# A recurrence in rounds: side work of three engines moved off the edges between rounds, and one masking operation for both heads

## The reference

```python
def step(state, inp):
    r_t, w_t, k_t, v_t, a_t, b_t = inp
    sa = jnp.einsum('bhvk,bhk->bhv', state, a_t)
    state = state * w_t[:, :, None, :] + sa[..., None] * b_t[:, :, None, :] + v_t[..., None] * k_t[:, :, None, :]
    y = jnp.einsum('bhvk,bhk->bhv', state, r_t)
    return state, y
...
y_f, bonus_f = direction(0)
y_b, bonus_b = direction(1)
y = y_f + y_b
mean = jnp.mean(y, axis=-1, keepdims=True)
var = jnp.mean(jnp.square(y - mean), axis=-1, keepdims=True)
yn = ((y - mean) * lax.rsqrt(var + RWKV_GN_EPS)).reshape(b, s, d) * lnx_w.astype(F32) + lnx_b.astype(F32)
out = (yn + (bonus_f + bonus_b).reshape(b, s, d)) * g.astype(F32)
```

## Time and profile before

| | |
|---|---|
| median of 3 runs | 2835.26 us (2833.51 to 2841.53) |
| profiled execution, its own time | 2841.87 us |
| its span | 2840.1 us |
| mean granted clock | 0.991 |
| PE busy | 2705.1 us (95%) |
| DVE, ACT, POOL busy | 1459.3, 1262.3, 1127.4 us |
| the recurrence | about from 787.3 to 1264.1 us of the span |

### The profile page before, as it was taken

One profiled execution on the slowest core, in us unless ns is written; L12 is line 12 of the kernel. 1 busy time (PEld: TensorE's weight loads), 2 busy tenths in 40 slices (PEclk: granted clock), 3 DMA queues, 4 the chain that ended last, 5 costly groups with the idle time before them and its releaser, 6 DMA issues.

```text
span 2840.1 us, 54966 instructions
## 1 busy us (share of the span) xinstructions
PE 2705.1 (95%) x23332; PEld 2152.4 (76%) x23332; DVE 1459.3 (51%) x2561; ACT 1262.3 (44%) x2296; POOL 1127.4 (40%) x634
## 2 busy tenths in 40 slices
PE   7999999979989999989999999899999999999999
PEld 5668888857777777777888877577777777788887
DVE  7956886056767777754888203712222224234410
ACT  5764434234556555544443325634444454422221
POOL 4124444533543333314444444043333443544443
PEclk9999999999999999999999999999999999999999
DMA  5112332322300000012233232032221322333322
GB/s 165 49 38 89 97 94 90 97 91 89 96 19 11 8 7 8 6 46 77 94 97 90 92 100 67 15 111 77 75 75 56 106 84 81 97 91 96 95 88 77
DMA packets 63460, 208.88 MB, mean 74 GB/s; under 512 B 11248, under 2 KB 11504, under 8 KB 62832
## 3 DMA queue, kind: packets, MB, share of 16 engines
q1 hardware_dynamic: 60704, 193.10, 22.0%
q0 software_dynamic: 1936, 10.91, 1.1%
q10 hardware_dynamic: 576, 1.35, 0.2%
HBM read 199.95 MB, written 4.19 MB: 72 GB/s over the span
## 4 chain that ended last, share of the span: by engine, by line
PE 83%; DVE 11%; ACT 3%; issue 2%; DMA 0%; POOL 0%; SPq 0%; DVEq 0%; ACTq 0%
PE banks L1672 22%; PE banks L1674 21%; PE banks L1673 21%; PE banks L779 6%; PE banks L788 1%; PE banks L1816 1%; DVE low L539 1%; ACT arena L1119 1%; DVE arena L1532 1%; DVE arena L2661 1%; PE banks L845 1%; PE banks L871 1%; PE banks L1709 1%; PE banks L1792 1%; PE banks L1864 1%
## 5 line engine op out<-in xcount | busy, mean ns | idle before, releaser
L312 POOL TENSOR_TENSOR low<-arena,high 128x1024 fp32r<-128x1024 f32 (+1 forms) x376 | 876.5, 2332 | 1323.3 <-ACT high L303 1320.0
L1672 PE MATMUL banks<-high,high 128*128 128x512 f32 (+1 forms) x2752 | 1093.5, 397 | 38.2 <-POOL low L312 21.2
L1674 PE MATMUL banks<-high,low 128*128 128x512 f32 (+1 forms) x2752 | 1082.4, 393 | 0.0
L1673 PE MATMUL banks<-low,high 128*128 128x512 f32 (+1 forms) x2752 | 1082.3, 393 | 0.0
L303 ACT ACTIVATE high<-arena 128x1024 fp32r<-128x1024 f32 (+1 forms) x376 | 382.0, 1016 | 802.6 <-PE banks L1674 801.3
L1672 PEld LDWEIGHTS banks<-high,high 128*128 128x128 f32 x2752 | 519.5, 189 | 170.0 <-POOL low L312 18.0
L1674 PEld LDWEIGHTS banks<-high,low 128*128 128x128 f32 x2752 | 519.4, 189 | 121.4
L1673 PEld LDWEIGHTS banks<-low,high 128*128 128x128 f32 x2752 | 519.9, 189 | 119.0 <-issue 1.9
L2556 DVE TENSOR_TENSOR arena<-banks,arena 128x512 f32<-128x512 f32 x48 | 33.1, 692 | 425.2 <-PE banks L1674 424.1
L779 PE MATMUL banks<-arena 64*64 64x64 f32 x5632 | 207.3, 222 | 37.1 <-ACT arena L1119 31.5
L2690 DVE SCALAR_TENSOR_TENSOR arena<-arena 128x511 f32<-128x511 f32 x88 | 237.2, 2695 | 3.1
(11 more groups left out here) (294 smaller groups left out, 2994.6 us busy)
## 6 DMA issues: line engine op xcount, KB each, us to landing
arena<-weights SPq DMA_DIRECT2D x302, 512.0 KB, 3.5
arena<-weights SPq DMA_DIRECT2D x48, 448.0 KB, 3.2
arena<-weights SPq DMA_DIRECT2D x28, 256.0 KB, 2.6
arena<-tables POOLq DMA_DIRECT2D x5, 448.0 KB, 3.7
arena<-x_t SPq DMA_DIRECT2D x4, 512.0 KB, 5.8
x_spill<-arena POOLq DMA_DIRECT2D x1, 2048.0 KB, 9.3
arena<-small_weights POOLq DMA_DIRECT2D x16, 128.0 KB, 2.7
arena<-x_spill POOLq DMA_DIRECT2D x1, 2048.0 KB, 8.8
```

The costliest lines, as they stand in the source:

```text
L312: pool.tensor_tensor(lo[:, 0:n], ring[w % RING][:, 0:n], hi[:, 0:n].bitcast(F32), ALU.subtract).then_inc(w_low, 1)
L1672: pe.matmul(dst, hi[:, c], x[0], start=kt == 0, stop=False)
L1673: pe.matmul(dst, hi[:, c], x[1], start=False, stop=False)
L1674: mm = pe.matmul(dst, lo[:, c], x[0], start=False, stop=kt == kts_of[t] - 1)
```

## The change

Five orders change and one operation is merged.

- VectorE: `exclusive` moves from the end of rounds 1 and 2 (behind the new state) to the step U5, behind `centre`. In round 3 `r_` goes ahead of `a_`: r_0 behind M, a_0 behind U2, r_1 behind U4, a_1 behind U5 (ahead of `y_out`).
- VectorE: both heads' NT are masked in one operation of 128x768 elements instead of two of 128x384 (`both_j` spans two PSUM banks).
- TensorE: `merge(i, 1)` goes ahead of `aux(i, 1)`.
- ScalarE: `sigmoid` of sa0 and sa1 and `shifted_bonus` move from ahead of the copies of S1 to behind those of S2; the exponentials of round 3 come later by a step, in the order er1, ei1, ea1, F.

```diff
-    PRE_ACT = ["ksq", "rn", "sw0", "sa0", "sw1", "sa1", "er0", "ea0", "ei0", "er1", "ea1", "ei1", "F"]
+    PRE_ACT = ["ksq", "rn", "sw0", "sa0", "sw1", "sa1", "er0", "ea0", "ei0", "er1", "ei1", "ea1", "F"]
...
-    INV_DVE = two("DT", "D", "M", "U2", "U3", "U4", "U5", "U6")
+    INV_DVE = ["DT"] + two("D", "M", "U2", "U3", "U4", "U5", "U6")
...
             if off:
+                merge(i, 1)
                 aux(i, 1)
-                merge(i, 1)
                 for h in range(2):
                     grow(i, h, 5)
                 aux_gate(i)
...
-                if c == 1 and more:
-                    sigmoid(j + 1, "sa0", PP[1])
-                if c == 2 and more:
-                    sigmoid(j + 1, "sa1", PP[1])
-                if c == 3 and j:
-                    shifted_bonus(j - 1, PP[1])
                 for h in range(2):
                     ev("S1", h, flat(R.P2[:, h, :, :]), 256)
...
                 for h in range(2):
                     ev("S2", h, flat(R.P4[:, h, :, :]), 256)
-                if c == 3 and more:
-                    factor(j + 1, "er1")
+                if c == 1 and more:
+                    sigmoid(j + 1, "sa0", PP[1])
+                if c == 2 and more:
+                    sigmoid(j + 1, "sa1", PP[1])
+                if c == 3 and j:
+                    shifted_bonus(j - 1, PP[1])
                 for h in range(2):
                     ev("S3", h, flat(R.D[:, h, :, :]), P)
                 if c == 0 and more:
                     norm_k(j + 1)
                 if c == 3 and more:
-                    factor(j + 1, "ea1")
+                    factor(j + 1, "er1")
...
                 if c == 3 and more:
                     factor(j + 1, "ei1")
-                    factor(j + 1, "F")
+                    factor(j + 1, "ea1")
                 for h in range(2):
                     ev("Q1", h, flat(R.P2[:, h, :, :]), 256)
...
+                if c == 3 and more:
+                    factor(j + 1, "F")
...
         def a_(j, d):
             ra.wait(dve, j, f"ea{d}")
-            dve.scalar_tensor_tensor(R.AR[j % 2][d][:, :, 0, :], c8(ea[d]), -1.0, c8(kkn), ALU.mult, ALU.mult)
+            rd.inc(dve.scalar_tensor_tensor(R.AR[j % 2][d][:, :, 0, :], c8(ea[d]), -1.0, c8(kkn), ALU.mult, ALU.mult), f"AR{d}")
 
         def r_(j, d):
-            rd.inc(dve.tensor_tensor(R.AR[j % 2][d][:, :, 1, :], c8(er[d]), c8(R.r[:, j, :]), ALU.mult), f"AR{d}")
+            ra.wait(dve, j, f"er{d}")
+            dve.tensor_tensor(R.AR[j % 2][d][:, :, 1, :], c8(er[d]), c8(R.r[:, j, :]), ALU.mult)
...
             elif at_ == (1, "U5") and more:
                 centre(j + 1, 0)
-            elif at_ == (1, "U6") and more:
                 exclusive(j + 1, 0)
...
             elif at_ == (2, "U5"):
                 if more:
                     centre(j + 1, 1)
+                    exclusive(j + 1, 1)
                 if j >= 2:
                     z_gate(j - 2, PP[1])
-            elif at_ == (2, "U6") and more:
-                exclusive(j + 1, 1)
             elif at_ == (3, "M") and more:
+                r_(j + 1, 0)
+            elif at_ == (3, "U2") and more:
                 a_(j + 1, 0)
-            elif at_ == (3, "U2") and more:
-                r_(j + 1, 0)
             elif at_ == (3, "U3") and prev:
                 y_normed(j - 1)
             elif at_ == (3, "U4") and more:
-                a_(j + 1, 1)
                 r_(j + 1, 1)
-            elif at_ == (3, "U5") and prev:
-                y_out(j - 1, PP[1])
+            elif at_ == (3, "U5"):
+                if more:
+                    a_(j + 1, 1)
+                if prev:
+                    y_out(j - 1, PP[1])
...
                 p2.wait(dve, i, "NT")
-                for h in range(2):
-                    d2.inc(dve.tensor_tensor(R.NM[:, h, :, :], PJ[h][:, 0:P].unsqueeze(1).to_broadcast([P, 3, P]), below, ALU.mult),
-                           f"DT_{h}")
+                d2.inc(dve.tensor_tensor(R.NM, both_j[:, :, 0:P].unsqueeze(2).to_broadcast([P, 2, 3, P]),
+                                         below.unsqueeze(1).to_broadcast([P, 2, 3, P]), ALU.mult), "DT")
```

More of the change, by code:

```diff
@@ L661, in build @@
     PI, PJ, PX, PP = psum[0:2], psum[2:4], psum[4:6], psum[6:8]
-    both_x, both_p = (banks[:, 1024 * k:1024 * k + 1024].rearrange("p (h b) -> p h b", h=2) for k in (2, 3))
+    both_j, both_x, both_p = (banks[:, 1024 * k:1024 * k + 1024].rearrange("p (h b) -> p h b", h=2) for k in (1, 2, 3))
     hf = lambda i: slice(64 * i, 64 * i + 64)
@@ L1106, in act_rwkv @@
                 copy(name, 7)
-                for n in ("er1", "ea1", "ei1", "F"):
+                for n in ("er1", "ei1", "ea1", "F"):
                     factor(0, n)
@@ L1460, in dve_rwkv @@
         for d in range(2):
+            r_(0, d)
             a_(0, d)
-            r_(0, d)
         wait_tile(dve, tiles_of["rw_g1"][-1])
@@ L1583, in dve_rwkv @@
                 new_state(1)
-            if off:
-                spread(i, "U6")
         y_bonus(KT - 1)
```

## The result

The changed kernel takes 2849.4 us, median of five runs (2846.29 to 2853.42), against 2835.9 before: ratio 1.0047, 95% interval 1.0036 to 1.0058. It is 13.5 us slower, where I had forecast 7 us faster. The profiled execution took 2853.42 us (span 2851.6), and the mean granted clock fell from 0.991 to 0.986.

What follows compares the result with a forecast made beforehand. TensorE, 83% of the chain of waits, was taken as the bound. 0.92 us for each of seven pairs gave 6.4, less 0.3 plus 0.9 made 7.0 us: from 2835.26 to 2828.3 us, range 2820 to 2836.

Steps and rivals of the forecast that it cites:

- In rounds 1 and 2 VectorE is later still, so nothing follows.: Moved sigmoids start `aux_left` and TensorE's queue behind it 0.1 to 0.2 us later; claimed cost in rounds 1 and 2: none.
- Rival 3, the clock: New idle ahead of merge drops the clock in all six gate rounds, 3.9 us each: 12 us slower, 2848; chance 0.06.
- the longest new idle stretch, some 0.6 us: Argument against clock falls: TensorE's new idle ahead of merge is no longer than what the other five gate rounds bore.
- The signs of being wrong: U5 later than merge + 1.5, merged mask over 1.0 us, round 3 longer, or clock falls in more than two rounds.
- The edges: Ends of rounds 1 and 2, where `exclusive` leaves the path: gains of 0.18 us into round 2, 0.39 into round 3.
- The sum per pair: Gain per pair of heads: 0.35 + 0.39 for edges and round 2, 0.13, -0.1 and 0.15 for rounds 0, 1, 3: 0.92 us.
- Round 0: Merge can start 0.6 us earlier, but a table load delays the copy of Q1: gain 0.13 us instead of 0.6.
- the shifted bonus: Moved behind the copies of S2 on ScalarE, it makes `aux_left` start later and costs 0.17 us in round 3.
- The merged mask: One VectorE operation takes some 0.9 us instead of 1.01 for two; hidden behind TensorE's own queue, so gain 0.
- Aux behind merge: Aux fills TensorE's wait for Q1 but outlasts it: U5 at merge + 1.4 to 1.5 us, against 1.17 before.
- Round 3: `r_1` takes 0.7 us ahead of GpSimd's L1236, `a_1` waits for L1237; U6 at 1084.7 against 1084.84, gain 0.15 us.
- The lock between VectorE and GpSimd: The operation that starts first blocks the other to its end; `y_square` meets 0.4 us less of it, U4 0.6 earlier.

Runs made afterwards that it cites:

- e1: Changed kernel with the sa0 and sa1 sigmoids back ahead of the copies of S1; 2828.07 us, 0.9966 of before.
- e4: Kernel before with only the two sigmoids moved behind the copies of S2; 2844.62 us, 1.0027 of before.
- e6: Changed kernel with five extra TensorE turns that nobody reads ahead of merge in rounds 1 and 2; 2831.83 us, 0.9985 of before.
- e2: Changed kernel with aux(i, 1) back ahead of merge(i, 1); 2830.91 us, 0.9984 of before.
- e14: Changed kernel with the sigmoids back and one extra, unneeded VectorE operation ahead of U4 in rounds 1 and 2; 2843.34 us, 1.003 of before.
- e3: Kernel before with only merge(i, 1) put ahead of aux(i, 1); 2839.28 us, 1.0011 of before.
- e10: Changed kernel with five extra TensorE turns that nobody reads ahead of merge in round 0 only; 2839.67 us, 1.0013 of before.
- e8: Kernel before with only `exclusive` moved from the end of rounds 1 and 2 to the step U5; 2829.16 us, 0.997 of before.
- e5: Changed kernel with both undone: sigmoids ahead of the copies of S1, aux(i, 1) ahead of merge(i, 1); 2825.61 us, 0.9962 of before.

## Why the prediction was wrong, by its own steps

- **The failed step: "In rounds 1 and 2 VectorE is later still, so nothing follows."** I followed the moved sigmoid to TensorE's `aux_left` only. GpSimd's `k_a` waits for it as well; I had its waits in the code, and had just used its collision with `y_square`. `k_a` started 2.8 us later in its round and held up the scan by 1.1 us (2.29 against 1.21). e1 undoes this alone: 1.1 us a pair and 21 us in all. e4 does it alone on the kernel before: 0.7 us more a pair, 7.6 us in all. So the 0 that I put down for the moved sigmoids in rounds 1 and 2 should have been a loss of 1.1 us a pair, more than the whole gain of 0.92.
- **Rival 3, the clock, at 0.06, was the case.** Its place, round 2, was right. That its 2848 us is so near the 2849.4 is luck, for two errors cancel: it took off 7 us of gain that did not come, and the five further falls cost less than 5 x 3.9 = 19.5 us (with a fall pairs 3 to 6 take 64.1, 64.2, 62.7 and 64.1 us against 59.9, but pairs 0 and 1 lose only some 1 and 2.5 us against e6). Nor did the six rounds with a gate all fall: pairs 2 and 7 did not, and pairs 0 and 1, which have none, did. Its chance rested on "the longest new idle stretch, some 0.6 us"; the stretch was 1.14 and 1.23 us, since the failed step and the swap of merge and aux add up. With the sigmoids back it is 0.64 us in round 2, as forecast, and 0.84 in round 1. e2, e6 and e14 show that the wait brings falls: taken by aux, filled, and made by other means. e3, e4 and e10 show that it is not all of the cause; what else decides stays open. The rule that windows run free of the kernel (the Trainium skill, TensorE: Matmul & The Clock Gate, "What's actually happening") made me call falls chance; but all five runs of the changed kernel had a clock of 0.986 to 0.988, so this was no chance of single runs.
- **The signs of being wrong** that the prediction named: the clock fell in six rounds of the recurrence and not in at most two; U5 starts later than merge + 1.5; round 3 of pair 4 is longer (14.6 us against 13.8), though not in pair 2, where no fall reaches into it (13.5).
- **The edges** were right. read_state to S1 of round 2 is 1.25 us (1.40 in the earlier trace rows). S1 of round 3 stands without idle time ahead of it, below, pair 2 of the changed kernel. e8 gives `exclusive` 0.5 us a pair.

```profile
954.01 0.43 PE L858 MATMUL banks<-arena 64*64 64x64 f32 x16
954.37 0.66 PE L711 MATMUL banks<-arena 128*128 128x128 f32 x4
954.96 1.15 PE L779 MATMUL banks<-arena 64*64 64x64 f32 x32
```

- **The sum per pair**, 0.92 us, is about what comes when the sigmoids are put back: 59.9 - 58.8 = 1.1 us (e1, e5), 8 us for seven pairs, and e1 is 8.9 us faster than before for the forecast 7.0. Its undisturbed rounds 1, 2 and 3 take 14.9, 16.3 and 13.5 us, for the forecast 15.0, 16.2 and 13.6. Round 0 gained 0.05 us and not 0.13, and the shifted bonus had the wrong sign.
- **The merged mask**: 0.95 us for an estimate of 0.9, hidden, as said.
- **Aux behind merge**: U5 starts 1.61 us after merge (1071.83 - 1070.22), 0.1 us more than the forecast 1.5, without idle time. But merge was not early in exchange.
- **Round 3.** `r_1` takes 0.68 instead of the 1.76 of the earlier trace rows, and `a_1` was held up as forecast and took 1.22 us; U6 follows `y_out` without idle time. Pair 4:

```profile
1090.06 0.68 DVE L1396 TENSOR_TENSOR arena<-arena 128x512 f32<-128x512 f32 x1
...
1092.44 1.22 DVE L1392 SCALAR_TENSOR_TENSOR arena<-arena 128x512 f32<-128x512 f32 x1
1093.58 0.74 DVE L1448 SCALAR_TENSOR_TENSOR arena<-banks,arena 128x512 f32<-128x512 f32 x1
1094.25 0.57 DVE L1533 TENSOR_TENSOR arena<-banks,arena 128x128 f32<-128x128 f32 x2
```

The lock between VectorE and GpSimd (the Trainium skill, SBUF — State Buffer, "Who interferes with whom") is what I took for `y_square` and then did not ask of the scan. The trace agrees once more: the scan ends at 1069.55, 1.09 us after L1230 does, and takes 1.21 us where nothing blocks it.

Pair lengths and clocks together give the times within about 4 us, with two exceptions. For the changed kernel: 0 for the pairs, (0.992 - 0.987) x 2840 = 14 us for the clock, 13.5 measured. For e5: -1.1 x 7 - 0.001 x 2840 = -11 us, -11.4 measured. The exceptions are e14, 12 us by this sum and 6 measured, and e10, 7 and 2.5; that stays open, as does what besides the waits shifts the falls.

## What to carry to other kernels

For each instruction that is moved later, list every engine that waits for its result, and look where their work then falls; an engine with 40% load can still collide with the one operation that is on the path. Where TensorE has filler work, put it where TensorE would wait, not behind: here 0.8 us of useless products in two rounds of each pair were worth 17.6 us. And when a forecast gives a clock fall a chance, work out the idle time of the whole new order first, since two moves that cost 2 and 8 us alone cost 24 us together (the changed kernel against e5).

## What the runs showed of the hardware

- Waits of 1.1 to 1.2 us of TensorE ahead of merge went with a clock fall in six of seven rounds 2 of the changed kernel; with 0.77 us of each filled (e6), with none. Such waits are not enough: e3 with 1.14 us in round 2 and e10 with both waits fell in two rounds 2 each. In pair 4 of the changed kernel the stretch at 1.2 GHz lay behind the wait, in the gate product and after it; pairs 0 and 1 fell without a gate product.
- The mean clock of single runs of one kernel scatters (0.983 to 0.993 in e14), and its time with it, 2859 to 2830 us: about 2.9 us for 0.001.
- A decay scan of 128x512 takes 1.21 us, and 2.29 us when an operation of GpSimd with two SBUF inputs had started first.
